# Gathering tokens from parts split once, in single fp32r passes, in a two-branch mixer and mixture-of-experts layer

## What is computed

```python
t = u.reshape(-1, d)                                   # 256 x 1024, u = rms_norm(h, ln2_w)
group_logits = (t @ w_group) + b_group                 # 4 groups, top 1
exp_logits = ((t @ w_expert) + b_expert)               # 4 experts per group, top 2
combine = ...                                          # weight of each token and expert
h_gate = jnp.einsum('td,edf->tef', t, w_gate)          # 16 experts, d_ff 512
h_up = jnp.einsum('td,edf->tef', t, w_up)
h = jax.nn.silu(h_gate) * h_up * combine[..., None]
y = jnp.einsum('tef,efd->td', h, w_down)
```

## Time and profile before

| | |
|---|---|
| runs | 915.78, 916.20, 919.01 us; median 916.2 us |
| span of the profiled execution, first to last instruction | 916.1 us |
| PE busy | 849.8 us (93%) |
| DVE, ACT, POOL busy | 628.4 (69%), 492.2 (54%), 157.3 us (17%) |
| mean granted TensorE clock | 0.978 of full |
| HBM read | 168.5 MB, 185 GB/s over the span |

### The profile page before, as it was taken

The page is one execution under the profiler, slowest core; times in us unless marked ns, Lnnn a source line. Parts: engine busy times, 40 slices in busy tenths (PEclk is TensorE's granted clock), DMA queues, the critical chain, the costliest instruction groups (busy, mean ns, idle before and its releaser), DMA issues.

```text
span 916.1 us, 15309 instructions
## 1 busy us (share of the span) xinstructions
PE 849.8 (93%) x5614; PEld 770.0 (84%) x5614; DVE 628.4 (69%) x792; ACT 492.2 (54%) x543; POOL 157.3 (17%) x216
## 2 busy tenths in 40 slices
PE   4999999998999999999879989999999999999993
PEld 2999999897998989989879987778878887887882
DVE  3599888555545556363697654899589769958973
ACT  5366555445444344443872332767486657748641
POOL 0012000008836748273040000000000000000000
PEclk9899999999999999999988999999999999999997
DMA  7254555222122122212252646389699968969931
GB/s 304 76 194 151 192 190 191 109 93 92 47 97 88 46 92 71 107 51 66 97 205 92 214 174 266 139 318 357 244 328 352 364 241 313 360 243 328 351 135 46
DMA packets 24478, 169.99 MB, mean 186 GB/s; under 512 B 2688, under 2 KB 3200, under 8 KB 4480
## 3 DMA queue, kind: packets, MB, share of 16 engines
q1 hardware_dynamic: 23024, 165.69, 50.0%
q10 hardware_dynamic: 1424, 3.90, 1.1%
HBM read 168.52 MB, written 1.05 MB: 185 GB/s over the span
## 4 chain that ended last, share of the span: by engine, by line
PE 73%; DVE 14%; issue 7%; ACT 5%; DMA 1%; DVEq 0%; ACTq 0%
PE ps L1309 11%; PE ps L1311 10%; PE ps L1310 10%; PE ps L1306 8%; PE ps L1307 8%; PE ps L1308 8%; PE ps L1495 4%; PE ps L1706 2%; DVE ldec L846 2%; DVE rawlo L721 2%; DVE moe_lo L1147 2%; PE ps L1544 1%; PE ps L1744 1%; PE ps L1384 1%; DVE hres L1141 1%
## 5 line engine op out<-in xcount | busy, mean ns | idle before, releaser
L1308 PE MATMUL ps<-act_r,rawlo 128*128 128x256 f32 x576 | 161.5, 280 | 0.0
L1308 PEld LDWEIGHTS ps<-act_r,rawlo 128*128 128x128 f32 x576 | 109.2, 190 | 0.0
L721 DVE TENSOR_TENSOR rawlo<-raw,whi 128x2048 fp32r<-128x2048 f32 x34 | 82.5, 2428 | 34.3 <-ACT whi L400 34.3
L1306 PE MATMUL ps<-act_r,whi 128*128 128x256 f32 x352 | 102.5, 291 | 1.8 <-DVE act_r L731 1.8
L1307 PE MATMUL ps<-act_r,whi 128*128 128x256 f32 x352 | 99.1, 281 | 0.0
L751 DVE SCALAR_TENSOR_TENSOR cacc<-ps,prm,cacc 128x255 f32<-128x255 f32 (+1 forms) x144 | 58.3, 475 | 24.0 <-ACT cacc L431 24.0
L1306 PEld LDWEIGHTS ps<-act_r,whi 128*128 128x128 f32 x352 | 67.3, 191 | 2.6 <-DVE act_r L731 2.6
L400 ACT CAST whi<-raw 128x2048 fp32r<-128x2048 f32 x34 | 64.7, 1902 | 5.4 <-PE ps L1311 5.4
L1307 PEld LDWEIGHTS ps<-act_r,whi 128*128 128x128 f32 x352 | 67.2, 191 | 0.0
L1310 PE MATMUL ps<-rawlo,xg 128*128 128x512 f32 x160 | 63.4, 396 | 0.0
L1309 PE MATMUL ps<-whi,act_r 128*128 128x256 f32 x192 | 57.7, 301 | 0.0
(11 more groups left out here) (357 smaller groups left out, 2498.9 us busy)
## 6 DMA issues: line engine op xcount, KB each, us to landing
raw<-w_mix SPq DMA_DIRECT2D x60, 1024.0 KB, 4.8
raw<-w_gate SPq DMA_DIRECT2D x24, 1024.0 KB, 5.2
moe_raw<-w_down SPq DMA_DIRECT2D x24, 1024.0 KB, 5.1
raw<-w_up SPq DMA_DIRECT2D x16, 1024.0 KB, 5.3
moe_raw<-w_up SPq DMA_DIRECT2D x16, 1024.0 KB, 5.4
moe_raw<-w_gate SPq DMA_DIRECT2D x8, 1024.0 KB, 5.9
raw<-w_down SPq DMA_DIRECT2D x8, 1024.0 KB, 5.2
xy<-x SPq DMA_DIRECT2D x1, 1024.0 KB, 6.9
```

What stands on the lines that cost most here:

```text
L721: dve.tensor_tensor(los[j], raw[:, j, :], f32(his[j % slots]), ALU.subtract).then_inc(lo_done, 1)
L1306: pe.matmul(dst, w_hi, a_hi, start=start, stop=False)
L1308: return pe.matmul(dst, w_lo, a_hi, start=False, stop=stop)
```

## The change

The tokens are split once, ahead of the first gather, into `u_parts`: part 0 is `u` times the norm factor, cast to fp32r by ACT (two activations of 128x1024, waiting for a new semaphore `n_r` of the norm factor), part 1 is the same product less part 0, by DVE (two instructions of 128x1024 in place of the scaling in place, each waiting for ACT's). Both are stored so that the 128 elements of a block k lie side by side; ACT and DVE read `u` with a step of eight elements for it. They lie in `act_r`, which is free by then. `gather` runs 16 fp32r matmuls on the high parts into banks 0 and 1 and then 16 on the low parts into banks 2 and 3, with a semaphore for each; `sel` becomes fp32r. `x_high` is unchanged; `x_low` becomes a plain copy of banks 2 and 3. The low half of the gather also waits until DVE has read the counts from bank 2 (`n_seen`) and until the low parts are there.

```diff
--- before.py
+++ after.py
@@ -151,6 +151,8 @@
 
         ht = xy_r[:, 1, :].rearrange("p (b i f s) -> p b i f s", b=2, i=2, f=4)
         u = xin
+        u_parts = [act_r[:, part, :, :].rearrange("p k s -> p (k s)").rearrange("p (t k s) -> p t k s", t=NT, k=KC)
+                   for part in range(2)]
         fin_out = xin
 
         front = ExitStack()
@@ -225,7 +227,7 @@
         hbuf = hs[:, 0:1024].rearrange("p (b f) -> p b f", b=2)
         sgate = hs[:, 1024:1536]
         ysp = sb("ysp", [P, 2, D], F32R)
-        sel = sb("sel", [P, NT, P])
+        sel = sb("sel", [P, NT, P], F32R)
         selt = sb("selt", [P, NT, P], F32R)
         cslot = sb("cslot", [P, EXPERTS])
         ln2b = sb("ln2b", [P, D])
@@ -290,7 +292,7 @@
                              "n_route"))
         e_sel, e_gath, e_xhi, e_xlo, e_silu, e_h, e_ht, e_hthi, e_htlo = (
             sem(n) for n in ("e_sel", "e_gath", "e_xhi", "e_xlo", "e_silu", "e_h", "e_ht", "e_hthi", "e_htlo"))
-        e_cs = sem("e_cs")
+        e_cs, e_glo, n_r, n_uh, n_seen = sem("e_cs"), sem("e_glo"), sem("n_r"), sem("n_uh"), sem("n_seen")
         n_init, n_cw = sem("n_init"), sem("n_cw")
         e_turn, e_back, e_zero = sem("e_turn"), sem("e_back"), sem("e_zero")
         e_yhi, e_ylo, e_scat, e_add = (sem(n) for n in ("e_yhi", "e_ylo", "e_scat", "e_add"))
@@ -634,6 +636,10 @@
                 for t in range(NT):
                     act.activation(act_r[:, t, 2 * i, :], hres[:, t, i * COLS:(i + 1) * COLS], ACT.Square,
                                    accum_out=stat[:, 5, i * NT + t:i * NT + t + 1]).then_inc(n_ss, 1)
+            act.wait_ge(n_r, 1)
+            for t in range(NT):
+                act.activation(u_parts[0][:, t, :, :], u[:, t, :].rearrange("p (s k) -> p k s", k=KC), ACT.Copy,
+                               scale=stat[:, 1, t:t + 1]).then_inc(n_uh, 1)
             act.wait_ge(n_lg, 1)
             act.activation(rt[:, 4, :, :], rt[:, 3, :, :], ACT.Exp).then_inc(n_exp, 1)
             act.wait_ge(n_lg, 2)
@@ -1046,7 +1052,8 @@
             dve.wait_ge(n_ss, 4 * NT)
             link(dve.tensor_reduce(stat[:, 0, 0:NT], stat[:, 5, 0:4 * NT].rearrange("p (i t) -> p t i", t=NT), AX_X,
                                    ALU.add))
-            rsqrt(NT, 1.0 / D, None)
+            rsqrt(NT, 1.0 / D, n_r)
+            dve.wait_ge(n_r, 1)
 
             R = [rt[:, i, :, :] for i in range(24)]
             io4 = iota[:, 0:4].unsqueeze(1).broadcast_to([P, NT, 4])
@@ -1084,7 +1091,10 @@
             dve.tensor_tensor(R[3], R[0], wide(1), ALU.subtract).then_inc(n_lg, 1)
             dve.wait_ge(n_ut, 4)
             for t in range(NT):
-                dve.tensor_scalar(u[:, t, :], u[:, t, :], stat[:, 1, t:t + 1], None, ALU.mult).then_inc(n_u, 1)
+                dve.wait_ge(n_uh, t + 1)
+                dve.scalar_tensor_tensor(u_parts[1][:, t, :, :], u[:, t, :].rearrange("p (s k) -> p k s", k=KC),
+                                         stat[:, 1, t:t + 1], f32(u_parts[0][:, t, :, :]),
+                                         ALU.mult, ALU.subtract).then_inc(n_u, 1)
 
             dve.wait_ge(n_cnt, 1)
             link(dve.tensor_tensor(R[23], ps[:, 2, 0:8].rearrange("p (t g) -> p t g", t=NT), R[2], ALU.mult))
@@ -1093,7 +1103,8 @@
             link(dve.tensor_reduce(col(22), R[23], AX_X, ALU.add))
             link(dve.tensor_scalar(qsl[:, :, 4:5], col(22), -1.0 - P, None, ALU.add))
 
-            link(dve.tensor_scalar(rinfo[:, 0:4], ps[:, 2, 8:12], float(P), None, ALU.is_gt))
+            dve.tensor_scalar(rinfo[:, 0:4], ps[:, 2, 8:12], float(P), None, ALU.is_gt).then_inc(n_seen, 1)
+            dve.wait_ge(n_seen, 1)
             link(dve.tensor_reduce(rinfo[:, 4:5], rinfo[:, 0:4], AX_X, ALU.add))
             link(dve.tensor_scalar(rinfo[:, 6:7], rinfo[:, 4:5], float(GROUPS), None, ALU.add))
             link(dve.tensor_tensor(rinfo[:, 0:4], rinfo[:, 0:4], iota[:, 0:4], ALU.mult))
@@ -1125,10 +1136,9 @@
 
                 dve.wait_ge(e_cs, it + 1)
                 dve.tensor_copy(cslot[:, :], ps[:, 7, 0:EXPERTS])
-                dve.wait_ge(e_xhi, it + 1)
-                dve.tensor_tensor(xg[:, 1, :, :].rearrange("p k s -> p (k s)"),
-                                  ps[:, 0:2, :].rearrange("p a b -> p (a b)"),
-                                  f32(xg[:, 0, :, :].rearrange("p k s -> p (k s)")), ALU.subtract).then_inc(e_xlo, 1)
+                dve.wait_ge(e_glo, it + 1)
+                dve.tensor_copy(xg[:, 1, :, :].rearrange("p k s -> p (k s)"),
+                                ps[:, 2:4, :].rearrange("p a b -> p (a b)")).then_inc(e_xlo, 1)
 
             def y_low(it):
                 dve.wait_ge(e_yhi, it + 1)
@@ -1700,15 +1710,21 @@
             pe.matmul(ps[:, 2, 8:12], ones, rt[:, 12, 0, :], start=True, stop=True).then_inc(n_cnt, 1)
             def gather(it):
 
+                def gather_part(part):
+                    for k in range(KC):
+                        for t in range(NT):
+                            ins = pe.matmul(ps[:, 2 * part + k // 4, (k % 4) * P:(k % 4 + 1) * P],
+                                            u_parts[part][:, t, k, :], sel[:, t, :], start=(t == 0), stop=(t == 1))
+                    return ins
+
                 pe.wait_ge(e_sel, it + 1)
-                for k in range(KC):
-                    for t in range(NT):
-                        ins = pe.matmul(ps[:, k // 4, (k % 4) * P:(k % 4 + 1) * P], u[:, t, k:D:KC], sel[:, t, :],
-                                        start=(t == 0), stop=(t == 1))
-                ins.then_inc(e_gath, 1)
+                gather_part(0).then_inc(e_gath, 1)
+                pe.wait_ge(n_seen, 1)
+                pe.wait_ge(n_u, 4 + NT)
+                gather_part(1).then_inc(e_glo, 1)
                 pe.wait_ge(n_cw, 1)
                 for t in range(NT):
-                    ins = pe.matmul(ps[:, 7, 0:EXPERTS], sel[:, t, :], cw[:, t, :], start=(t == 0), stop=(t == 1))
+                    ins = pe.matmul(ps[:, 7, 0:EXPERTS], f32(sel[:, t, :]), cw[:, t, :], start=(t == 0), stop=(t == 1))
                 ins.then_inc(e_cs, 1)
 
             def scatter(it, t):
@@ -1724,7 +1740,7 @@
                                         start=(part == 0), stop=(part == 1))
                 ins.then_inc(e_scat, 1)
 
-            pe.wait_ge(n_u, 4 + NT)
+            pe.wait_ge(n_uh, NT)
             gather(0)
             pe.wait_ge(n_route, 1)
             runs = pe.value_load(rint[0:1, 0:1], min_val=GROUPS, max_val=GROUPS + 1)
@@ -1745,7 +1761,7 @@
                         ins.then_inc(e_ht, 1)
                     if n == TURN_SEL:
                         for t in range(NT):
-                            ins = pe.transpose(ps[:, 7, (t + 1) * P:(t + 2) * P], sel[:, t, :], ident)
+                            ins = pe.transpose(ps[:, 7, (t + 1) * P:(t + 2) * P], f32(sel[:, t, :]), ident)
                         ins.then_inc(e_turn, 1)
                     if n == NEXT_GROUP:
                         pe.wait_ge(e_back, it + 2)
```

## The result

The changed kernel takes 908.9 us (median of 4 runs, 907.91 to 910.94); before, beside it, took 917.4 us (4 runs, 915.78 to 919.01). The ratio is 0.9897 (95% interval 0.9875 to 0.9920): faster by 1.0%. The prediction was 905.4 us within 902 to 909, and 1.2% less. The device time of an execution isn't its span: the one profiled here took 909.67 us with a span of 907.6, and the gap is 2.0 to 2.2 us in every other profiled run whose own time is known.

A forecast was written before the change was run, and what follows sets the result against it. PE was taken to bound the expert loop, with DVE's chain leading ahead of it. From 916.1 us, 11.85 saved in three gathers and 1.1 added ahead of the loop gave 905.35, forecast as 905.4, range 902 to 909.

The forecast's parts named there:

- The gather in the loop: Gathers in the expert loop: contiguous blocks cut 7.50 us to 3.55 each, saving 11.85 for three.
- The lower end of the range: Gathers in the loop: a pitch near 0.08 us a pass, giving 902.6 us.
- What hides behind it: Behind the shorter gather in the loop: DVE keeps 2.7 us of slack, ACT 4.8, so nothing comes late.
- the added waits: PE's two new waits in the loop, on low parts and counts read: nothing, at most some 0.1 us.
- Ahead of the loop: DVE's work on `u` before the loop: two instructions at 1.283 us replace two in 1.41, +1.1 on the chain.
- the sum: Whole kernel: 916.1 - 11.85 + 1.1 = 905.35 us against the profiled span, 905.4 as median.
- Instructions of over 2 us at the split: Sign of a wrong forecast: ACT or DVE instructions that long where `u` is split ahead of the loop.
- rival A: Ahead of the loop: strided reads of `u` slow ACT and DVE by 2.1, +4.0 rather than +1.1, 908.3 us; 10%.
- Rival C: Start of the loop: piece 0 at half clock takes 2.8 us more, partly covered, about 907 us; 6%.
- Rival D: Behind each gather in the loop: PE falls to 1.2 GHz, losing 8.3 us per gather, 930.3 us; 3%.
- B: Gathers in the loop: columns set the pitch, the load hides, 1.84 us each, 900.3 us; 7%.
- E: Gather: fp32r passes keep the old pitch and only +1.1 is left, 917.3 us; 1%.

The follow-up runs named there:

- experiment 1: Kernel before, with ACT scaling `u` into contiguous float32 blocks, DVE's scaling left out and no fp32r in the gather: 907.26 us, ratio 0.9864.
- experiment 2: Changed kernel with its parts in natural order, the fp32r gather reading every eighth element: 928.69 us, ratio 1.0114.
- Experiment 7: Changed kernel with DVE's two low-part instructions issued twice, the first time into a free buffer: 910.53 us (one run).
- experiment 3: Changed kernel with DVE's low split moved from ahead of the counts to behind the combine weights: 913.4 us, ratio 0.9942.
- experiment 5: Changed kernel with four idle float32 matmuls of 512 columns between the counts and the first gather: 909.67 us, ratio 0.9902.
- experiment 6: Kernel before, with the float32 gather's stationary operand at steps of 4 and 2 elements, output not the reference's: 912.22 us (one run).

## Why the prediction was right, and where it wasn't

- **The gather in the loop.** Worked out as 3.55 us, measured 3.52; the three save 11.8, worked out as 11.85. The lower end of the range, a pitch near 0.08, was not seen. That the step of 32 bytes made the pitch, and not the type, was an inference from rows of other matmuls; experiments 1 and 2 show it by changing one and not the other.
- **What hides behind it.** Slack of 2.7 and 4.8, measured 3.14 and 4.95. The pass shrank by all that the gather gave, and nothing in the loop shows a cost of the added waits, as said.
- **Ahead of the loop.** Here a term of the sum was mis-sized. The prediction had two DVE instructions at 1.28 in place of 1.41 for both, +1.1. They take 2.06 each and the front stretch lost 2.4. Instructions of over 2 us at the split are one of the signs that the prediction itself had named as "wrong". The mechanism was named as rival A (strided reads cost on ACT and DVE too, 10%) and set aside since no row of before showed a large strided read there. It should have been the forecast: the only operation seen with that step paid for it, and nothing excluded it for the others. Its factor of 2.1 was too high, though: ACT's copies rose by 1.9 (1140 to 2141 ns), DVE's by 1.6 (1281 to 2062), which is why 2.4 and not 4.0 were lost. What was said against A, that four operations pay the step once where the gather paid it 128 times over, counts loads against operations; by elements it is 4 x 1024 against 4 gathers x 32 passes x 128, a fourth. Of the 2.4, 1.6 are the step (experiment 2), and the other 0.9 answer to the +1.1 of the sum. Experiment 7 shows that what DVE's splits take more lies on the chain, and experiments 1 and 3 that without them PE's counts bound the chain instead.
- **Rival C** (a cold start of the loop): the fall of the clock came, some 13 us at 1.2 GHz (0.51 in the stretch above), and its price was nothing that can be seen rather than 1.6 (experiment 5). Piece 0 starts at 588.03, 0.24 behind the end of `x_low`, and only its first matmul is slow: the next one follows 0.77 later, where it does after 0.33 in experiment 5. From the end of `x_low` to the next gather it is 66.80 us in before and 66.79 in after, so the first pass lost nothing by it.
- **Rival D** (the clock falls behind each gather in the loop) didn't happen in the changed kernel, but experiment 2 shows that it was near: the same single passes at the old pitch lose the clock. What the prediction said against it, that new and old gather stream in the same share of their time, is borne out as far as that goes.
- **B and E** are excluded by the pitch of 0.110.
- The sum with the terms as measured: 916.1 - 11.8 + 2.4 = 906.7, and 0.7 of drift in the mixer plus 0.2 at the end make the 907.6 of the profile. The medians of after, 908.9, 909.1 and 909.9, beside medians of before of 917.4, 918.9 and 919.1, lie 0.1 under the upper bound of the range, and above it; the saving in them is 8.4 to 9.8, where 10.8 was forecast. Of the 3.5 us between 905.4 and 908.9, some 2.4 are that smaller saving (8.4 for 10.8), and 1.2 the starting level, which was 916.2 in three runs and 917.4 in the four beside after. That the time lies within the range is thus in part luck; it lies nearer to rival A's 908.3 than to the forecast, and only the rows tell that A's mechanism was at work, at its smaller size.

## What to carry to other kernels

Look at the step of every operand ahead of its type: a stationary operand that is read every eighth float32 costs twice as much as a contiguous one, and laying it out once gave this change all it gained. The re-layout pays the same step once, so it belongs on the engine off the chain (ACT here) and not on the one that leads (DVE here). Where an edit thins out what PE streams, read the granted clock behind it: one layout of the same parts kept it, the other lost it for 6.8 us a gather.

## What the runs showed of the hardware

- The pitch of the gather's passes by the step of the stationary operand, at full clock: 0.110 us contiguous, 0.118 at 8 bytes, 0.225 at 16, 0.234 at 32; contiguous and at 32 bytes for float32 and fp32r alike, the two between on float32 only. The Trainium skill (SBUF — State Buffer, Door 1: The DMA port swizzle) says that a line has 16 bytes and wants two hits, and that one can stride 4 float32 for free. The first agrees with experiment 6; the second doesn't hold for this gather, since a step of 4 (16 bytes) cost nearly everything.
- The 0.225 isn't shown for every short matmul. The turn of the product (line 1744), one record a matmul, has a stationary operand with a step of 16 bytes too, and its four loads in the timeline of PE's weight loads of before take 681.10 to 681.57, 0.12 each. Why it is spared was not tried.

```profile
681.10 0.56 PEld L1744 LDWEIGHTS ps<-cst,hs 128*128 128x128 f32 x4 [1.61 <-DVE hs L1168]
681.57 0.20 PEld L1309 LDWEIGHTS ps<-moe_hi,xg 128*128 128x128 f32 x1
```

- The clock matters little to a strided pass: in experiment 2 the gather takes 7.49 us, nearly half of it at 1.2 GHz, and before's takes 7.50 at full clock. Contiguous passes go from 0.110 to 0.214.
- The load sets the pace of these short matmuls, and not the moving columns: the step of the stationary operand alone changes the pitch, and it is 0.11 with 48 moving columns as with 128. The contiguous pitch, 0.110, is close to what the Trainium skill (TensorE: Matmul & The Clock Gate, LDWEIGHTS) gives for a load of 128 columns, by estimate 128 / 1.2 = 107 ns.
- A step of 32 bytes on reads of 128x1024 float32 cost ACT 1.0 us and DVE 0.8 us per instruction; a step of 512 bytes on ACT's write side cost 0.9.
- A gather in which PE counts as busy all the time lost its clock for 6.8 us with single fp32r passes at 0.234 (0.52 in the row above), while the float32 gather of the same duration in the loop, whose passes carry their columns twice, kept it at 1.00. Busy time on the page doesn't tell the two apart. What exactly does was not settled.
